# Hybrid attention and PEER layer: a ring of six double slots in the last stage, half the score buffer, and x read from PSUM

## The reference

```python
h = h + memory_attention(rms_norm(h, norm_mem_q), rms_norm(mem, norm_mem_kv), ...)
xn = rms_norm(h, norm_ffn)
s = einsum('chpd,hpnd->chpn', (xn @ w_q), sub_keys)       # scores, 2 lists of 128 for each head
top_s, top_i = top_k(s, 16); best_s, best_j = top_k(sums of pairs, 16)
a = gelu(einsum('cd,chkd->chk', xn, u_tab[expert]))       # 128 dots of 1024 for each token
h = h + einsum('chk,chkd->cd', softmax(best_s) * a, v_tab[expert])
out = rms_norm(h, norm_final)
```

## Time and profile before

| | |
|---|---|
| median of three runs | 4223.93 us |
| profiled execution, its own time | 4242.59 us |
| its span | 4240.8 us |
| TensorE clock granted, mean | 0.926 |
| busy: PE, DVE, ACT, POOL | 3325.1, 2173.1, 1296.3, 1568.2 us |
| bytes moved | 1288.22 MB, 304 GB/s over the span |
| chain that ended last | DMA 22%, PE 16%, DVE 6%, ACT 4%, issue 4% |

### The profile page before, as it was taken

The page is one execution under the profiler, slowest core; times in us unless marked ns, Lnnn a source line. Parts: engine busy times, 40 slices in busy tenths (PEclk is TensorE's granted clock), DMA queues, the critical chain, the costliest instruction groups (busy, mean ns, idle before and its releaser), DMA issues.

```text
span 4240.8 us, 33463 instructions
## 1 busy us (share of the span) xinstructions
PE 3325.1 (78%) x9134; PEld 1565.7 (37%) x9134; DVE 2173.1 (51%) x4954; ACT 1296.3 (31%) x3390; POOL 1568.2 (37%) x1367
## 2 busy tenths in 40 slices
PE   8589989658776788878786887788778768976776
PEld 6545455323333454444332332233233223322222
DVE  0311122177567677667238447545744674485444
ACT  1011123111112343333133433433343343343333
POOL 0000000055544666667323344334423433344453
PEclk9899987789998999999898999999999999999999
DMA  7610031599988899989878899989989998999998
GB/s 283 237 39 22 22 114 56 183 354 386 330 298 311 329 360 382 340 316 372 353 250 309 339 371 373 361 331 377 377 327 362 369 374 337 373 380 368 379 381 327
DMA packets 283599, 1288.22 MB, mean 304 GB/s; under 512 B 27424, under 2 KB 52128, under 8 KB 192928
## 3 DMA queue, kind: packets, MB, share of 16 engines
q0 software_dynamic: 195120, 1073.83, 66.9%
q1 hardware_dynamic: 83696, 195.62, 12.6%
q10 hardware_dynamic: 4608, 16.78, 1.1%
HBM read 1243.13 MB, written 42.99 MB: 303 GB/s over the span
## 4 chain that ended last, share of the span: by engine, by line
DMA 22%; PE 16%; DVE 6%; ACT 4%; issue 4%; DVEq 0%; SPq 0%; POOLq 0%; ACTq 0%
DMA s_ring<-peer_uv,s_expert 15%; PE e_acc L405 11%; PE e_product L1635 5%; DMA e_more_slots<-peer_uv,s_expert 4%; DVE s_ring L331 2%; ACT s_diagonal L275 1%; DMA s_ring<-peer_v,s_expert 1%; ACT s_gate L288 1%; DMA s_x<-next_x 1%; DMA next_h<-e_work 1%; DMA e_work<-norm_ffn_row 1%; ACT s_dots L286 1%; ACT L286 0%; DVE e_work L1476 0%; DVE e_more_slots L331 0%
## 5 line engine op out<-in xcount | busy, mean ns | idle before, releaser
L405 PE MATMUL e_acc<-s_ring,s_diagonal 128*128 128x512 f32 x2676 | 1368.8, 639 | 497.3 <-ACT s_diagonal L275 406.0
L331 DVE CUSTOM_DVE_ANT_0 s_ring<-s_ring,s_x 128x1024 f32<-128x1024 f32 x886 | 1081.0, 1222 | 821.2 <-DMA s_ring<-peer_uv,s_expert 614.3
L244 POOL DMA_INDIRECT s_ring<-peer_uv,s_expert x555 | 656.7, 1183 | 1046.1 <-PE e_acc L405 667.8
L405 PEld LDWEIGHTS e_acc<-s_ring,s_diagonal 128*128 128x128 f32 x2676 | 499.1, 199 | 1313.0 <-ACT s_diagonal L275 745.5
L244 POOL DMA_INDIRECT s_ring<-peer_u,s_expert x331 | 368.2, 1113 | 392.4 <-DVE s_expert L1579 235.5
L286 ACT ACTIVATE s_dots<-s_dots 128x1 f32<-128x1 f32 x704 | 142.0, 202 | 1158.5 <-DVE s_dots L331 1157.6
L244 POOL DMA_INDIRECT s_ring<-peer_v,s_expert x327 | 369.3, 1129 | 336.1 <-PE e_acc L405 117.8
L275 ACT ACTIVATE s_diagonal<-s_ident,s_gate 128x128 f32<-128x128 f32 x1024 | 396.7, 398 | 291.3 <-PE e_acc L405 177.1
L405 PE MATMUL e_acc<-e_more_slots,s_diagonal 128*128 128x512 f32 x568 | 279.4, 615 | 75.9 <-ACT s_diagonal L275 73.5
L405 PE MATMUL a_acc<-s_ring,s_diagonal 128*128 128x512 f32 x426 | 247.4, 688 | 106.8 <-DMA s_ring<-peer_v,s_expert 47.2
L244 POOL DMA_INDIRECT e_more_slots<-peer_uv,s_expert x138 | 161.3, 1169 | 240.6 <-PE e_acc L405 183.1
(11 more groups left out here) (203 smaller groups left out, 3345.6 us busy)
## 6 DMA issues: line engine op xcount, KB each, us to landing
e_halves<-peer_scores SPq DMA_DIRECT2D x12, 2048.0 KB
e_halves<-mem_scores SPq DMA_DIRECT2D x6, 2048.0 KB
e_halves<-mem_values SPq DMA_DIRECT2D x6, 2048.0 KB
s_ring<-peer_uv,s_expert POOLq DMA_INDIRECT x555
p_w_in<-w_in SPq DMA_DIRECT2D x8, 1104.0 KB
f_w_big<-w_mem_kv SPq DMA_DIRECT2D x4, 2048.0 KB
f_w_big<-peer_w_q_t SPq DMA_DIRECT2D x2, 4096.0 KB, 17.8
peer_scores<-f_stage_s SPq DMA_DIRECT2D x16, 512.0 KB, 3.6
```

Source lines behind the costliest of these rows:

```text
L244: pool.indirect_dma_start(out=to, out_offset=None, in_=table, in_offset=bass.IndirectOffsetOnAxis(ap=self.expert[c % PICK_BUFFERS][:, k:k ...
L331: dve.tensor_tensor_reduce(row, row, self.x[:, :], 1.0, 0.0, ALU.mult, ALU.add, self.dots[:, k:k + 1]).then_inc(self.u_used, 1)
L405: last = pe.matmul(self.acc[:, at:at + BANK], self.diagonal[:, made % DIAGONALS, :], row[:, at:at + BANK], start=(n == group[0]), stop=(n ...
```

## The change

Four things change.

1. In the last stage the ring has 12 slots, six double slots, instead of 10.
2. Two buffers change. `b.work` of the last stage has half its size: groups 0 and 2 share one half, 1 and 3 the other. `keep_2` and `keep_3` move to the late steps, behind group 0 and behind group 1. And `s_x` is freed with the attention's buffers: in the last stage x is loaded into `s_scratch`, ten rows before the chunk's first dot, and ACT copies it from there to PSUM (`e_x_copy`) when the last dot of the chunk before is made. Then DVE reads it from PSUM. The first stage (chunk 0) has the copy too, from `s_x`. `end_root` waits until the next chunk's x is copied.
3. At the entry of the last stage (row 640) x of chunk 2, whose rows go on there, is loaded again into `s_scratch` and copied.
4. PSUM for `e_x_copy` comes from `e_turned`, which is now `e_product1`; the output products of the memory attention go to `e_product0`. PE waits for three more things: the four copies of the chunk before ahead of its first transposes, the softmax ahead of the output products, h2 ahead of the scores.

```diff
-WIDE_RING = 10
+X_AHEAD = 10
+WIDE_RING = 12
...
+        for s, (start, until, mode) in enumerate(self.stages):
+            first = next(n for n in range(start, until) if ROWS[n][0] == "u")
+            c = ROWS[first][1] // PICKS
...
+            if mode == "pe":
+                self.copy_x_at[start] = c
...
+                if start <= LAST_U[c - 1] < until:
+                    self.load_x_at[LAST_U[c - 1] + 1 - (X_AHEAD if mode == "pe" else 0)] = c
...
+                        self.copy_x_at[LAST_U[c - 1] + 1] = c
... scalar()
+            x = self.scratch if s == len(self.stages) - 1 else self.x
+            if n in self.load_x_at:
+                c = self.load_x_at[n]
                 act.wait_ge(self.x_kept[c], 32)
-                act.wait_ge(self.u_used, PICKS * c)
-                act.dma_start(self.x[:, :], self.io["next_x"][c]).then_inc(self.x_loaded, 16)
+                if self.mode(n) == "pe":
+                    act.wait_ge(self.x_copied, self.copies[s, c - 1])
+                    need(act, self.out_stored, 16 * (c - 1))
+                else:
+                    act.wait_ge(self.u_used, PICKS * c)
+                act.dma_start(x[:, :], self.io["next_x"][c]).then_inc(self.x_loaded, 16)
+            if n in self.copy_x_at:
+                c = self.copy_x_at[n]
+                if x is self.scratch and self.first_in(s) == c:
+                    act.wait_ge(self.out_stored, 16 * self.ended(n))
+                    act.dma_start(x[:, :], self.io["next_x"][c]).then_inc(self.x_loaded, 16)
+                act.wait_ge(self.x_loaded, 16 * self.x_loads[s, c])
+                if self.copies[s, c] > 1:
+                    act.wait_ge(self.u_used, PICKS * c)
+                act.activation(self.x_copy[:, :], x[:, :], ACT.Copy).then_inc(self.x_copied, 1)
... end_root()
+        if c + 1 < CHUNKS and LAST_U[c] >= self.stages[-1][0]:
+            act.wait_ge(self.x_copied, self.copies[len(self.stages) - 1, c + 1])
... vector()
+                if k == 0 or n in self.first_u:
+                    if copied:
+                        dve.wait_ge(self.x_copied, self.copies[s, c])
...
+                x = self.x_copy if copied else self.x
+                dve.tensor_tensor_reduce(row, row, x[:, :], 1.0, 0.0, ALU.mult, ALU.add,
... pick_buffers(), pick_chunks()
-    b.work = sb("e_work", [P, 2 * D])
+    b.work = sb("e_work", [P, D if resident else 2 * D])
+    b.work_groups = 2 if resident else 4
-    b.turned = ps("e_turned", [P, D])
+    b.turned = b.product[1]
+        stream.x_copy = ps("e_x_copy", [P, D])
+        def work_of(g):
+            at = g % b.work_groups
+            return b.work[:, BANK * at:BANK * (at + 1)]
-                    "out_a": (b.product[1][:, 0:BANK], b.mem_out), "out_b": (b.product[1][:, BANK:D], b.mem_out)}
+                    "out_a": (b.product[0][:, 0:BANK], b.mem_out), "out_b": (b.product[0][:, BANK:D], b.mem_out)}
... keep
+                    if g < b.work_groups:
+                        need(act, b.step, PICK_STEPS * (f - 1) + GROUP_STEPS * (g + 1 + 4 - b.work_groups))
+                    else:
+                        act.wait_ge(b.step, PICK_STEPS * f + GROUP_STEPS * (g + 1 - b.work_groups))
... PE
+                    if n == 0:
+                        need(pe, b.scores_kept, 4 * f)
-                        need(pe, b.scores_kept, 4 * f)
+                        pe.wait_ge(b.mem_exped, MEM_HEADS * (f + 1))
+                        pe.wait_ge(b.h2_ready, f + 1)
... order of the steps
+def late_beside_keeps():
+    group = len(LATE_STEPS) // 4
+    return (LATE_STEPS[:group] + ["keep_2"] + LATE_STEPS[group:2 * group] + ["keep_3"] + LATE_STEPS[2 * group:])
```

More of the change, by code:

```diff
@@ L101 @@
 CHUNK_END = {c: V_AT[PICKS * (c + 1) - 1] for c in range(CHUNKS)}
-LOAD_X_AT = {U_AT[PICKS * (c + 1) - 1] + 1: c + 1 for c in range(CHUNKS - 1)}
+LAST_U = [U_AT[PICKS * (c + 1) - 1] for c in range(CHUNKS)]
+X_AHEAD = 10
 RING = 8
-WIDE_RING = 10
+WIDE_RING = 12
 DIAGONALS = 3
@@ L132, in __init__ @@
         self.ring = sb("s_ring", [P, RING, D])
+        self.x = sb_early("s_x", [P, D])
         self.more_slots = None
         self.acc = None
+        self.x_copy = None
         self.row_loaded = [sem(f"s_row_loaded{i}") for i in range(WIDE_RING)]
@@ L177, in __init__ @@
             last_in[slot] = n
+        self.load_x_at, self.copy_x_at, self.copies, self.first_u, self.x_loads = {}, {}, {}, set(), {}
+        last_stage = len(self.stages) - 1
+        for s, (start, until, mode) in enumerate(self.stages):
+            first = next(n for n in range(start, until) if ROWS[n][0] == "u")
+            c = ROWS[first][1] // PICKS
+            self.first_u.add(first)
+            self.x_loads[s, c] = max(self.x_loads.values(), default=0) + (s in (0, last_stage))
+            if mode == "pe":
+                self.copy_x_at[start] = c
+                self.copies[s, c] = len(self.copies) + 1
+            for c in range(1, CHUNKS):
+                if start <= LAST_U[c - 1] < until:
+                    self.load_x_at[LAST_U[c - 1] + 1 - (X_AHEAD if mode == "pe" else 0)] = c
+                    self.x_loads[s, c] = 1 + max(self.x_loads.values())
+                    if mode == "pe":
+                        self.copy_x_at[LAST_U[c - 1] + 1] = c
+                        self.copies[s, c] = len(self.copies) + 1
         used = [0] * WIDE_RING
@@ L241, in gpsimd @@
             if paired:
-                to = self.ring[:, slot:slot + 2, :] if slot < RING else self.more_slots[:, :, :]
+                to = self.ring[:, slot:slot + 2, :] if slot < RING else self.more_slots[:, slot - RING:slot - RING + 2, :]
                 to = to.rearrange("p s d -> p (s d)")
@@ L277, in scalar, with first_in, ended @@
         self.at["scalar"] = max(until, self.at["scalar"])
+    def first_in(self, s):
+        return ROWS[next(n for n in range(self.stages[s][0], len(ROWS)) if ROWS[n][0] == "u")][1] // PICKS
+    def ended(self, n):
+        return sum(at < n for at in self.end_store_at)
     def coeff_alone(self, g):
@@ L327, in vector @@
             if kind == "u":
-                if k == 0:
-                    dve.wait_ge(self.x_loaded, 16 * (c + 1))
+                s = self.stage_of[n]
+                copied = self.mode(n) == "pe"
+                if k == 0 or n in self.first_u:
+                    if copied:
+                        dve.wait_ge(self.x_copied, self.copies[s, c])
+                    else:
+                        dve.wait_ge(self.x_loaded, 16 * self.x_loads[s, c])
                 self.wait_row(dve, n)
-                dve.tensor_tensor_reduce(row, row, self.x[:, :], 1.0, 0.0, ALU.mult, ALU.add,
+                x = self.x_copy if copied else self.x
+                dve.tensor_tensor_reduce(row, row, x[:, :], 1.0, 0.0, ALU.mult, ALU.add,
                                          self.dots[:, k:k + 1]).then_inc(self.u_used, 1)
@@ L1433, in step @@
                         act.wait_ge(b.x_ready, f + 1)
-                    need(act, b.step, PICK_STEPS * (f - 1) + GROUP_STEPS * (g + 1))
-                    act.activation(b.work[:, BANK * g:BANK * (g + 1)],
+                    if g < b.work_groups:
+                        need(act, b.step, PICK_STEPS * (f - 1) + GROUP_STEPS * (g + 1 + 4 - b.work_groups))
+                    else:
+                        act.wait_ge(b.step, PICK_STEPS * f + GROUP_STEPS * (g + 1 - b.work_groups))
+                    act.activation(work_of(g),
                                    b.product[g // 2][:, BANK * (g % 2):BANK * (g % 2 + 1)], ACT.Copy).then_inc(b.scores_kept, 1)
@@ L1524, in step @@
                     four = range(4 * g, 4 * g + 4)
-                    top_16(part, [b.work[:, PEER_KEYS * i:PEER_KEYS * (i + 1)] for i in four], [b.top[:, i, :] for i in four],
+                    top_16(part, [work_of(g)[:, PEER_KEYS * i:PEER_KEYS * (i + 1)] for i in range(4)], [b.top[:, i, :] for i in four],
                            [b.top_at[:, i, :] for i in four])
@@ L1543, in step @@
                     pairs = TOPK * TOPK
-                    top_16(part, [b.work[:, pairs * h:pairs * (h + 1)] for h in two], [b.best[:, h, :] for h in two],
+                    top_16(part, [work_of(g)[:, pairs * h:pairs * (h + 1)] for h in range(2)], [b.best[:, h, :] for h in two],
                            [b.best_at[:, TOPK * h:TOPK * (h + 1)] for h in two])
@@ L1688, in chained, with one_by_one @@
     return events
-def one_by_one(starts, until):
+def one_by_one(starts, until, halved=False):
     events = []
+    early = EARLY_STEPS + [name for name in peers_beside_keeps() if not halved or name not in ("keep_2", "keep_3")]
+    late = late_beside_keeps() if halved else LATE_STEPS
     for f, (start, stop) in enumerate(zip(starts, starts[1:] + [until])):
         turn = start + (stop - start) * 55 // 100
-        events += spread(EARLY_STEPS + peers_beside_keeps(), f, start, turn) + spread(LATE_STEPS, f, turn, stop)
```

(1 more changed line is left out.)

19 lines of the change are left out of this document (9 added, 10 removed).

## The result

| | before | after |
|---|---|---|
| median on one chip | 4228.25 us (4222.44 to 4236.24) | 4088.78 us (4084.10 to 4093.07) |
| ratio, 95% interval | | 0.9667 [0.9646, 0.9688] |
| profiled execution, its own time; span | 4242.59; 4240.8 | 4086.41; 4084.6 us |
| busy PE, DVE, ACT, POOL | 3325.1, 2173.1, 1296.3, 1568.2 | 3284.0, 2166.0, 1300.4, 1374.5 us |
| bytes moved, over the span | 1288.22 MB, 304 GB/s | 1288.75 MB, 316 GB/s |

The median before is here that of four runs; the forecast had the first three, 4223.93 us. Forecast were 4190 us, from 4158 to 4234. The change brought four times the 34 us forecast: 140 us of the medians, 156 of the two spans. The same bytes are moved at a higher rate, and POOL is busy 194 us less.

A forecast was written before the change was run, and what follows sets the result against it. Gathers (DMA) were taken to bound second parts of chunks and the end, PE first parts; 10 + 11 + 5.6 + 6.3 + 5 - 4 = 34 us saved gave 4190 us, range 4158 to 4234.

The forecast's parts named there:

- Direction and plan of the chunk: Last stage: gathers bound a chunk's second part, PE its first; five slots give 2.76 us a pair; 34 us faster overall.
- Rival A: Last stage: the sixth slot gives nothing, as DMA is full and PE bounds elsewhere; 4217 us; chance 0.20.
- B: Last stage: small loads wait behind outstanding gathers, a sixth slot adds 44 us; 4234 or 4240 us; chance 0.13.
- C: DMA reaches 0.99 over the whole 1876 us, PE-bound first parts shrinking too; 75 us less 4, 4153 us; chance 0.10.
- The failed step: Sixth slot in DMA-bound stretches: 0 to 0.055 us for each of 365 pairs, 0 to 20 us, taken as 10.
- x in PSUM: Last stage's dots reading x from PSUM take 1217 ns against 1221 from SBUF; nothing gained (0 to 0).
- Stalls: Sixth slot keeps DMA fed while rows stall: 11 us after the gain's wait, 5.6 between softmax and gain, over four chunks.
- x ahead: x loaded ten rows early: 2.1 us at each of three chunk changes, 6.3 us, plus 5 at the last change.
- Entry: At row 640, reloading and copying x beside the table loads delays PE's rows: 4 us lost (0 to 33).
- Moved copies and shared buffers: Score copies of groups 2 and 3 moved to the second part, PSUM shared: nothing, a loss up to 1 us x 10.

## Why the prediction was wrong

**Direction and plan of the chunk: right.** Gathers bound the second part, PE the first, and the ring's loop was at the pace that five slots give. Rival A is out (pace 2.50, not 2.76), B too (small transfers no slower). C was on the right side but stopped at 4153 us, and its mark didn't show: the first part shrank by 3 us, not by over 6. None of the rivals reached 4089.

**The failed step: "DMA is at 0.98 at that pace, so its own floor is 0.98 x 2.76 = 2.70."** The share adds up the times in which packets are open, and some packets stay open far longer when the ring is short of slots. The kernel with four slots shows 0.96 at 367 GB/s, 343 ns for a packet; before it is 0.98 at 383 and 335 ns, after 1.01 at 419 and 316 ns. The 2% seen as idle were 9% of the rate. The floor is 2.49 to 2.52 us: all kernels of six and eight slots stop there. Half of the packets took 309 ns before the change already, which makes 2.47 us for a pair; 6.4% of them took over 400 ns. What such a packet waits for, no view shows. For the 365 pairs of the forecast, 0.26 us in place of 0.027 are 2.76 - 2.50 = 0.26, x 365 = **95 us in place of 10**. With that alone the sum would be 119 us, 4240.8 - 119 = 4122 on the span. The evidence against 2.70 was in the forecast's own row: 383 GB/s in a stretch called full, where its estimate for the entry used 420 GB/s. Nor was the term bounded by it: "0 to 20" took both ends from the share.

**x in PSUM, "nothing (0 to 0)".** Right for the dot (1217 ns as forecast), wrong for its neighbour. POOL's gathers were held beside dots with both inputs in SBUF, 1103 ns before against 943 after, and the timeline of before had a shorter one, 0.94 us: a spread that should have been asked after. With five slots that is worth 56 us, with six nothing. So neither "the ring" nor "PSUM" is the cause of the 95 us by itself: either would have fed DMA better, and together they don't add up. From before: 26 us for all the rest, then 56 for PSUM and about 66 to 75 for the slot (0.9823 less 0.9667 or 0.9646, of 4228), or 124 for the slot and none for PSUM.

**Stalls, 11 + 5.6 us.** Not measured by themselves. POOL's idle time at the change of chunk went from 11.44 to 9.85 us, 1.6 us less where 2.7 were forecast, and two slots more on top of six bring 27 us by the ratios. With x in SBUF the pace (2.72 to 2.51 us, 365 pairs) explains 77 of the sixth slot's 124 us, so what is left, 47 us, is more than 16.6. Whether it is stalls or pairs of the first parts is open.

**x ahead, 6.3 + 5 us.** x loaded late costs 9 to 12 us of the last stage, 14 to 23 by the ratios: the size is about right. The form was right too: h1's wait stands beside x's. The one change of chunk compared gave 1.0 us, not 2.1.

**Entry, -4 us.** 0. x came later than estimated (16.5 us for 13), but PE's rows don't bound this stretch: it is as long as before to 0.4 us.

**Moved copies and shared buffers, 0.** This isn't shown. All that isn't ring or PSUM brings 26 us by the ratio (0.5% [0.3, 0.7]) and 36 by the last stage, where 7 were forecast. Five slots with x in SBUF are 13.4 and 12.9 us shorter than before from the third load of h1 to the fourth and to the fifth, where the late load of x cost nothing with six slots, and 11.5 us shorter behind it. So part of this gain has probably another source than the early load, and these edits weren't undone by themselves.

## What to carry to other kernels

A DMA share near 1 says that packets are open, not that the engines are full: take the GB/s beside it and compare with the best rate of the same packets anywhere in the trace, before you call a ring's depth useless. When an instruction of POOL has a shortest and a longer duration, look for what runs on VectorE beside the longer ones; moving one operand to PSUM may free it. Two edits that feed the same starved resource don't add up; undo each by itself before giving either the credit. And check in the trace that a delay which you put in delays the instruction after it: here 0.68 us of pause moved it by 0.03.

## What the hardware showed that I had not expected

- The share reads 0.96 at 367 GB/s, 0.98 at 383 and 1.01 at 416 to 421, all for 8 KB packets of gathers. Half of these packets take 309 to 312 ns in each case; 9.0% take over 400 ns at 367 GB/s, 6.4% at 383, 0.4% at 419.
- A gather instruction takes 0.94 us, and up to 1.97 us beside a dot of 1.23 us with both inputs in SBUF; with one of them in PSUM it stays at 0.94. With six slots and SBUF its mean near the end was 1.80 us (212.87 / 118) at an undiminished 417 GB/s. The Trainium skill (SBUF — State Buffer, SBUF: two separate sides) has the two engines share a pair of ports by a lock that one holds for a whole instruction, VectorE also for one with two SBUF inputs beside a GpSimd instruction that reads SBUF. The trace agrees as to the gather: the held one ended 0.82 us after its dot, about its own 0.94. It doesn't show the lock on VectorE: a dot that began 0.58 us behind a gather's start took 1.23 us as ever.
- With x in SBUF and five slots, gathers began no later after PE's last matmul (0.80 us), but their dots began 8.53 us behind them in place of 7.73, and that cost 56 us. The mean gather instruction was only 0.29 us longer; why the data came 0.80 us later is open, as no view shows when descriptors are written.
- A clearing of 128x256 by POOL and a wait for it, put ahead of a gather, made it begin 0.03 us later: 0.80 us lie between PE's last matmul and the gather without it, 0.83 with it.
- A copy of 128x1024 by ACT from SBUF to PSUM takes 1.03 us; its square of the same size into SBUF took 1.04.
